# Rotary embedding: the exchanged halves come from copies on ACT's DMA queue instead of TensorE products

## The reference

```
def _rope(x, positions):
    ...
    x1, x2 = jnp.split(x.astype(jnp.float32), 2, axis=-1)
    out = jnp.concatenate([x1 * cos - x2 * sin, x2 * cos + x1 * sin], axis=-1)
    return out.astype(x.dtype)
...
    qc = _rope(cq.reshape(b, s, N_HEADS, HEAD_DIM), positions)
    kc = _rope(ck.reshape(b, s, SWA_KV_HEADS, HEAD_DIM), positions)
...
        q = rope(rmsnorm(q, q_norm[l]))
        k = rope(rmsnorm(k, k_norm[l]))
```

## Time and profile before

| | us |
|---|---|
| median of 3 runs | 1780.29 |
| lowest, highest | 1778.01, 1781.07 |
| the profiled execution | 1775.64 |
| its span (first to last instruction) | 1773.6 |
| PE busy in the span | 1698.6 |
| DVE, ACT, POOL busy | 779.4, 695.1, 677.5 |

### The profile page before, as it was taken

The page is one execution under the profiler, slowest core; times in us unless marked ns, Lnnn a source line. Parts: engine busy times, 40 slices in busy tenths (PEclk is TensorE's granted clock), DMA queues, the critical chain, the costliest instruction groups (busy, mean ns, idle before and its releaser), DMA issues.

```text
span 1773.6 us, 24207 instructions
## 1 busy us (share of the span) xinstructions
PE 1698.6 (96%) x8858; PEld 1336.3 (75%) x8858; DVE 779.4 (44%) x1496; ACT 695.1 (39%) x1144; POOL 677.5 (38%) x523
## 2 busy tenths in 40 slices
PE   6999999999999979989999999999998999999999
PEld 5876568787666857867888888878776888888887
DVE  7226564402656264674455115532565365403540
ACT  4444462534445152554343224333354344313431
POOL 3432215443311642425443444345152534434443
PEclk9999999999999979989999999999898999999999
DMA  7320103222110211212222232222121222232222
GB/s 255 106 72 28 69 25 120 96 96 72 49 49 25 84 48 48 73 49 81 101 95 85 89 104 95 82 98 96 49 73 49 95 95 95 74 116 96 95 78 88
DMA packets 24608, 145.90 MB, mean 82 GB/s; under 512 B 3152, under 2 KB 3536, under 8 KB 10704
## 3 DMA queue, kind: packets, MB, share of 16 engines
q1 hardware_dynamic: 21840, 138.01, 22.7%
q10 hardware_dynamic: 2688, 6.82, 1.0%
HBM read 142.72 MB, written 2.10 MB: 82 GB/s over the span
## 4 chain that ended last, share of the span: by engine, by line
PE 68%; issue 19%; POOL 7%; DVE 3%; ACT 2%; DMA 1%; POOLq 0%; ACTq 0%; DVEq 0%
PE ring L520 59%; POOL w_lo L506 7%; PE outs L580 2%; PE scores L566 1%; PE ring L566 1%; PE scores L590 1%; PE ring L604 1%; PE ring L590 1%; PE ring L660 1%; DMA xt<-in_x 1%; PE ring L922 1%; PE ring L634 1%; DVE g L1737 0%; ACT xh L1253 0%; ACT xt L1249 0%
## 5 line engine op out<-in xcount | busy, mean ns | idle before, releaser
L506 POOL TENSOR_TENSOR w_lo<-w_stage,w_hi 128x258 fp32r<-128x258 f32 (+5 forms) x471 | 643.9, 1397 | 1053.0 <-ACT w_hi L1026 652.2
L520 PE MATMUL ring<-xh,w_lo 128*128 128x512 f32 x1296 | 518.0, 400 | 25.0 <-DVE w_lo L1444 10.6
L520 PE MATMUL ring<-xh,w_hi 128*128 128x512 f32 x1296 | 511.9, 395 | 0.0
L520 PE MATMUL ring<-xl,w_hi 128*128 128x512 f32 x1296 | 511.6, 395 | 0.0
L520 PEld LDWEIGHTS ring<-xh,w_lo 128*128 128x128 f32 x1296 | 244.9, 189 | 87.2 <-DVE w_lo L1444 10.6
L520 PEld LDWEIGHTS ring<-xh,w_hi 128*128 128x128 f32 x1296 | 244.8, 189 | 55.4
L520 PEld LDWEIGHTS ring<-xl,w_hi 128*128 128x128 f32 x1296 | 245.2, 189 | 53.0
L1375 ACT ACTIVATE w_hi<-w_stage 128x2048 fp32r<-128x2048 f32 (+2 forms) x70 | 116.6, 1666 | 158.8 <-PE ring L520 158.8
L1385 ACT ACTIVATE g<-ring,convw 128x512 f32<-128x512 f32 x88 | 68.1, 778 | 245.4 <-DVE ring L1876 245.4
L1026 ACT ACTIVATE w_hi<-w_stage 128x2064 fp32r<-128x2064 f32 (+2 forms) x81 | 123.5, 1537 | 92.7 <-PE ring L520 92.1
L1858 DVE TENSOR_TENSOR xt<-xt,ring 128x512 f32<-128x512 f32 x48 | 33.0, 688 | 248.2 <-PE ring L520 248.2
(11 more groups left out here) (288 smaller groups left out, 2255.8 us busy)
## 6 DMA issues: line engine op xcount, KB each, us to landing
w_stage<-in_mixed SPq DMA_DIRECT2D x62, 1032.0 KB, 4.8
w_stage<-in_up SPq DMA_DIRECT2D x44, 1024.0 KB, 4.8
w_stage<-in_down SPq DMA_DIRECT2D x16, 768.0 KB, 4.2
w_stage<-in_down SPq DMA_DIRECT2D x16, 640.0 KB, 3.9
xt<-in_x ACTq DMA_DIRECT2D x4, 512.0 KB, 11.3
out_t<-xt ACTq DMA_DIRECT2D x8, 256.0 KB, 2.0
mem_f<-in_mem SPq DMA_DIRECT2D x1, 1024.0 KB, 9.5
bias_r<-in_relb SPq DMA_DIRECT2D x1, 1024.0 KB, 11.5
```

Source lines behind the costliest of these rows:

```text
L506: ins = nc.gpsimd.tensor_tensor(w_lo[:, slot, cols], source[:, cols], w_hi[:, slot, cols].bitcast(F32), ALU.subtract)
L520: ins = nc.tensor.matmul(o, lhs, rhs, start=start, stop=stop, skip_group_check=True)
```

## The change

The signed permutation is replaced by a plain copy with the halves exchanged, made by DMAs from SBUF to SBUF on ACT's queue (`swap_halves`); the sign goes into the sine tables (the frequencies of block 1 and the sine table of block 2 carry a minus for the first half). `rope` multiplies the copy by the sine in place. A tile of 128 rows takes four DMAs of 32 rows (64 KB each, or 128 KB each for the two q tiles that go together in block 2), the rows 64 to 95 two DMAs of 16 rows. The copies lie in `tmp` in block 1 and in `g` in block 2. All 26 rotation products, their ring banks, and the two constant matrices go. The units of block 1 are numbered anew (`until`): 61 where there were 64, with three units in each of the first four steps where it was six, and cv in four parts instead of two.

```
@@ b1_units
-    units += [[("lat_q", l), ("lat_kv", l)], [("rot", l, "ck"), ("rot", l, "kr")]] + [[], [], [], [("w", l, "cq1")]]
-    units += [[("rot", l, "cq0")], [], [("w", l, "cv")], [("rot", l, "cq1")]]
+    units += [[("lat_q", l), ("lat_kv", l)]] + [[], [], [], [("w", l, "cq1")]] + [[], [], [], [("w", l, "cv")]]
...
-    for name in ("uv", "uq", "rotq"):
+    for name in ("uv", "uq"):
@@ units_in_step
-    return 3 if block == 1 and t < 6 else 2
+    return 3 if block == 1 and t < 4 else 2
@@ PE
-                for t in range(4):
-                    wait_taken(pe, ("q", l, t))
-                    rotate(("rq", l, t), rot64, q2[:, t, :])
                 begin_chunk(c0 + 3)
@@ ACT
+            def swap_halves(dst, src, rows, half, name):
+
+                for first in range(rows.start, rows.stop, 2 * half):
+                    for a, b in ((first, first + half), (first + half, first)):
+                        act.dma_start(dst[a:a + half], src[b:b + half]).then_inc(S(name), 16)
...
+                    yield from until(17)
                     round_chunk(b1_chunk(l, 9), half=1)
+                    wait_taken(act, w("ck"))
+                    swap_halves(tmp[:, 3, :], kc[:, :], slice(0, P), 32, "ck_swapped")
+                    swap_halves(tmp[:, 2, :], raw[:, 1, :], slice(64, 96), 16, "kr_swapped")
...
+                    yield from until(26)
+                    round_chunk(b1_chunk(l, 10), half=0)
+                    wait_taken(act, w("cq1"))
+                    swap_halves(tmp[:, 1, :], qc[:, 1, :], slice(0, P), 32, "cq1_swapped")
+                    yield from until(27)
+                    round_chunk(b1_chunk(l, 10), half=1)
...
+                    yield from until(37)
+                    for h in range(4):
+                        wait_taken(act, ("uq", l, h))
+                    act.wait_ge(S("rope_done"), 11 * l + 7)
+                    swap_halves(tmp[:, :, :], qb[:, :, :], slice(64, 96), 16, "uq_swapped")
...
                     if t in (1, 3):
                         round_chunk(b2_chunk(l, 2 + t // 2))
+                        for n in (t - 1, t):
+                            wait_taken(act, ("q", l, n))
+                        swap_halves(g[:, t - 1:t + 1, :], q2[:, t - 1:t + 1, :], slice(0, P), 32, f"q_swapped{t // 2}")
+                wait_taken(act, ("k", l))
+                swap_halves(g[:, 4, :], k2[:, :], slice(0, P), 32, "k_swapped")
@@ DVE
+            def rope(swapped, x, rows, cosine, sine, outs, sem):
+
+                v.tensor_tensor(swapped, swapped, sine[rows, :], ALU.mult).then_inc(S("sine_part"), 1)
+                sines_done[0] += 1
                 step(v.tensor_tensor(x, x, cosine[rows, :], ALU.mult))
+                dve.wait_ge(S("sine_part"), sines_done[0])
                 for dst in outs:
+                    v.tensor_tensor(dst, x, swapped, ALU.add).then_inc(S(sem), 1)
...
+                for t in range(3):
+                    scaled(t)
+                rotated(0)
+                rotated(1)
+                scaled(3)
+                scaled(4)
+                rotated(2)
+                rotated(3)
                 name = ("v", l)
                 wait_full(dve, name)
                 v.tensor_tensor(tmp[:, 3, :], bank(name)[:, :], tmp[:, 0, :], ALU.mult).then_inc(freed(name), 1)
+                rotated(4)
```

More of the change, by code:

```diff
@@ L185, in ring_plan @@
         take(("q", l, 3), ("k", l), ("v", l))
[L186 removed]
+        for b, name in ((2, ("tv2", l)), (3, ("hms", l)), (0, ("u", l, 0, 0)), (1, ("u", l, 1, 0)), (4, ("k_bc", l))):
+            take_on(b, name)
         interleave(pairs_block2(l), fourier_units(l), 2)
@@ L655, in transpose_all @@
                 ins.then_inc(S("ring_full"), 1)
-            def rotate(name, rot, x, rows=slice(0, P)):
-                o = acquire(name)
-                nc.tensor.matmul(o[rows, :], rot[rows, :], x, start=True, stop=True, skip_group_check=True).then_inc(S("ring_full"), 1)
             def later_projections(l, c0):
@@ L732, in later_projections @@
                     r3(o[0:96, :], w_hi[0:64, c % 2, w1], w_lo[0:64, c % 2, w1], lat_h[0:64, 1, :], lat_l[0:64, 1, :], False, True, True)
-                    if h % 2 == 1:
-                        yield
-                for h in range(4):
-                    wait_taken(pe, ("uq", l, h))
-                    rotate(("rotq", l, h), rot32, qb[64:96, h, :], slice(64, 96))
                     if h % 2 == 1:
@@ L1588, in later_projections, with until @@
                 def later_projections():
-                    def idle(n):
-                        for _ in range(n):
+                    slot = [0]
+                    def until(n):
+                        while slot[0] < n:
+                            slot[0] += 1
                             yield
-                    yield from idle(16)
+                    yield from until(16)
                     wait_taken(dve, ("lat_ms", l))
                     v.reciprocal(rtok[:, :], stat[:, :]).then_inc(S("lat_inv"), 1)
-                    yield
-                    yield from idle(4)
+                    yield from until(21)
                     name = ("lat_q", l)
@@ L1612, in later_projections @@
                     dve.sem_inc(freed(name), 1)
-                    yield
-                    rope(("rot", l, "ck"), kc[:, :], full, cos64, sin64, [kc[:, :]], "rope_done")
-                    dve.wait_ge(S("rope_done"), 11 * l + 1)
-                    rope(("rot", l, "kr"), raw[rr, 1, :], rr, cos32, sin32, [kb[rr, h, :] for h in range(4)], "rope_done")
-                    yield
-                    yield from idle(2)
+                    yield from until(22)
+                    dve.wait_ge(S("ck_swapped"), 64 * (l + 1))
+                    rope(tmp[:, 3, :], kc[:, :], full, cos64, sin64, [kc[:, :]], "rope_done")
+                    dve.wait_ge(S("kr_swapped"), 32 * (l + 1))
+                    rope(tmp[rr, 2, :], raw[rr, 1, :], rr, cos32, sin32, [kb[rr, h, :] for h in range(4)], "rope_done")
+                    yield from until(25)
                     dve.wait_ge(S("pv_done"), 64 * l + 16)
@@ L1745, in _, with scaled @@
                 dve.wait_ge(S("tables_loaded"), 32)
-                for t in range(5):
+                def scaled(t):
                     name = ("q", l, t) if t < 4 else ("k", l)
```

159 lines of the change are left out of this document (58 added, 101 removed).

## The result

The change makes the kernel slower: 1805.28 us median (1803.65 to 1814.19) against 1779.74 of the kernel before in the same comparison, a ratio of 1.0154 (95% interval 1.0120 to 1.0189). The prediction said 1762.3, with a range from 1747 to 1773. The profiled execution took 1805.62 us, its span is 1803.2, 29.6 more than before.

The account below looks back on a forecast made before the run. PE (TensorE), busy 1698.6 of 1773.6 us, was taken to bound the kernel. Gains of 16.8 us in block 1 and 1.2 in block 2 make 18.0: 1775.64 - 18.0 = 1757.6, plus 4.65, 1762.3 us; range 1747 to 1773.

Parts of the forecast that it names:

- What goes from PE: Block 1, per layer: rotation products and waits leave PE, gaining 4.01 + 0.95 + 1.5 + 6.85 us.
- The bursts of B's ropes: Block 1: twelve DVE operations of four query ropes in two successive steps cost 1.4 us a layer, bounds 0 and 3.
- The rope reads SBUF where it read PSUM: DVE's rope operations: reading SBUF instead of PSUM takes 0.68 us either way, so costs 0.
- ck and kr: Block 1: their nine DVE rope operations make PE wait 2.1 us a layer, bounds 0 and 3.
- cq1: Block 1: its product gives 0.95 us, plus 0.55 of PE's 0.80 wait behind it: 1.5 a layer, bounds 0.95 and 1.75.
- ACT's issues: Block 1: six copy issues ahead of a pair of exponentials, 2.0 us, half hidden, cost 0.7 us a layer.
- The clock behind rotq: Block 1: small records and work behind the rotq products run at full instead of half clock, gaining 1.5 us a layer.
- Issues at 0.34 us: ACT's queue: each issue of a copy was taken to cost 0.34 us.
- rival 1: Issues hold up ACT at 0.97 us each: 21 us lost in all, 1783 us; decides from 0.88 per issue; chance 0.09.
- v 2.7 us later: Block 2: two rounds of copies and four ropes ahead of v cost PE 2.7 us a layer, bounds 0.7 and 6.
- The clock in block 2: Block 2: after a longer pause the forty small products lose 1.5 us a layer at half clock, bounds 0 and 3.
- Rival 2: Block 2: copies land late; at 7.4 us no gain is left, at 10 us 1790 us; chance 0.07.

Follow-up runs that it names:

- e1: The change with block 2's queries, key and v all scaled on DVE before the five ropes: 1779.14 us.
- e8: The kernel before with the copies in block 2 alone, v scaled before the ropes, block 1 keeping its PE products, units and order: 1767.87 us.
- e7: e5 with cq1's rope on DVE two units later (unit 34 instead of 32): 1759.02 us.
- e3: The change with the four ropes of B's queries in block 1 one per attention step instead of two and two: 1797.19 us.
- e5: The change with the edits of e1 and e3 together: 1768.34 us.
- e4: A separate small program without the kernel's work, timing DVE and copies: two SBUF operands 0.61 us alone, 1.08 beside POOL; an issue 0.61 us.
- e9: The change with only cq1's rope two units later (unit 34 instead of 32): 1799.38 us.
- e6: The change with two DMAs of 64 rows per 128-row tile instead of four of 32, rotary embedding not computed: 1802.74 us.
- e2: The change with v's scaling ahead of only the last two query ropes in block 2: 1794.94 us in one run.

## Why the prediction was wrong, step by step

The sum was 16.8 us gained in block 1 and 1.2 in block 2. It was wrong in both blocks, and in the sign of each. The runs give 12 lost in block 1 (e1 against e8) and 13 lost in block 2 (26 for the order, by e1, less 13 that the copies are worth in a good order, by e8).

- *"What goes from PE".* Right in kind. The rotations are gone, and with ropes that stand well both parts gain, 9 us and 13 us (e7, e8).
- *The bursts of B's ropes, 1.4 us a layer, bounds 0 and 3.* This step failed in block 1, in its path and so in its size: 3.9 us of waits go when the ropes are spread (e3), 2.8 of them for a gate's bank, and 3.4 us of clock (0.17 of 20 us) stood behind them. I followed DVE's lateness to the scores only; it also goes through the exponentials on ACT to the ring banks that ACT frees. Spreading the ropes gives 8 us (e3) or, with v first, 12 (e5 against e1).
- *"The rope reads SBUF where it read PSUM, 0.68 either way: 0".* This failed beside it. It is 0.68 us only while POOL rests; beside a split it is 0.8 to 1.24, and the cosine and sum have that risk too. By the durations it adds 1.1 us to cq1's rope and 1.8 to the first pair of B's in each layer; how much of the 12 us that makes is not separated from the place of the ropes ahead of the maxima. The rows of before could hardly show it, since the one operation of a layer that met a split read a bank; the section of the Trainium skill that is named under e4 would have. The renumbering and the free timing of copies put the ropes of cq1 and B beside splits.
- *ck and kr, a wait of 2.1.* Measured 0.7, before the scores at 162 us: inside the bounds of 0 and 3.
- *cq1, 0.55 of the 0.80 for POOL.* POOL's wait stays at 0.7, and 1.9 for vb comes with it. I had looked for ACT's issues in this place; DVE's rope was the cause (e9, e7): moving it gives 6 us alone and 9 on top of e5.
- *ACT's issues, 0.7, and the new slot order, 0.7.* The first is not on the path (e6); the second was not tested by itself.
- *The clock behind rotq, 1.5 us.* Right there (1.00 from 200 to 220 us, 0.91 before) and given back in the next 20 us (0.83 where it was 1.00). The clock falls behind another wait instead.
- *Issues at 0.34 us.* Wrong, 0.61. By rival 1's own rule that is 9 us less gain (0.27 / 0.63 of 21), not all of it. But the rival, which made this decide, is no cause in block 1 (e6), nor in block 2 when v is ahead (e1). Inside the chain ahead of v it counts, 1.7 us a layer as worked out next.
- *Block 2, "v 2.7 us later".* This is the step that failed in block 2. The chain was drawn right and nearly each link was too short. From the second scaling on, with its own times: the first ropes start 3.3 us later than the chain said (the last of four issues starts 1.9 us after the scaling and not 1.0, and lands 5.8 us later and not 3.5), take 6.9 and not 4.1, and the second copies come 3.1 later (the last issue after 1.9 and not 1.1, a landing of 4.9 and not 2.6); the last two ropes take 3.9. That is 9 us, and v waits 12.3 where 3.5 was written. The upper bound of 6 was too low because it let only the landing vary. e2 and e1 show that the order makes it: 26 us in all, where 2.7 and 1.5 us a layer stood.
- *The clock in block 2, 1.5 us a layer.* Too small in the first layer, right in the second: v's transposes to the first scores were to fall by 3.8 and 2.8 us and fell by 1.5 (21.3 to 19.8) and 2.9 (22.0 to 19.1). Against the kernels with v first the stretch is about 3 us longer in each layer.
- *The wait before the first scores, 1.0 back in the first layer.* Right: 0.9 us where 1.99 stood.
- *Rival 2, copies land late.* Partly true: 4.6 of the 9 us are landings, which is about 9 us in two layers by the rival's own rule. The prediction's own sign for being wrong, a landing of 5 us or more, came. It matters only inside the chain; with v first the copies of the query tiles land after 3.8 us in the median and delay nobody (e1).

The chances were the last mistake: the chain ahead of v was named "the weak place", and I priced it for a good case in every link.

What stays open: how much each fall of the clock costs. e8 has block 1 unchanged, and its profile is 4 us behind the kernel before at the end of the first layer, with 0.83 of the clock from 200 to 220 us against 0.91. The profile of e1, whose block 1 is the change's, is 14 us behind at the end of that block where the change's is 9. So stage by stage a single profile is good to some 5 us; the sums above rest on medians. Open too is why even e7 gains 9 us in block 1 where 16.8 stood: waits of 3.0 us for a gate's bank stay in each layer, and the kernel before has none. And the 2.2 us ahead of DVE's scaling of q0 were not followed up.

## What to carry to other kernels

When work leaves TensorE for DVE's memory, look up for each new DVE operation where both operands lie and what POOL does at that moment: with two SBUF operands it cost mostly 1.1 to 1.2 us beside POOL here where it cost 0.6 to 0.7 alone, and a place two units away can be free. Scale and release what TensorE waits for first, and let round trips of copies run behind it; one in the chain cost TensorE nearly 5 us of wait here, two 11.5. And count what a late engine holds up: two ropes in one step delayed the maxima more than the split beside them did. Follow a late DVE through ACT to the banks that ACT frees, and look at the next 20 us of the clock behind every wait that you make or take away.

## What the runs showed of the hardware

- POOL suffers too: its subtraction of 128 x 258 took 722 to 1279 ns in e4, and a split of eight pieces 7.9 us beside two ropes in the change against 5.65 in e1.
- A copy within SBUF lands after 2.0 us alone, and a group of four of 128 KB after 6.0 beside a load of 1 MB.
- Taking a wait away gave more than the wait: 9.3 us in e7 for two waits of 1.9 us; the granted clock around the first of them was higher too (1.00 from 180 to 200 us, 0.83 in e5).
